# GpSimd's turns of an expert stage, thirty of them written out and without marks

## The reference

```python
def expert_block(args):
    xb, e = args
    gu = xb @ w_gate_up[e] + b_gate_up[e]
    gate = jnp.minimum(gu[:, 0::2], SWIGLU_LIMIT)
    up = jnp.clip(gu[:, 1::2], -SWIGLU_LIMIT, SWIGLU_LIMIT)
    act = (up + 1.0) * gate * jax.nn.sigmoid(SWIGLU_ALPHA * gate)
    return act @ w_down[e] + b_down[e]
...
out = jnp.zeros((T, D), jnp.float32).at[row_tok].add(ys.astype(jnp.float32) * row_w[:, None])
```

## Time and profile before

| | |
|---|---|
| median of three runs | 1679.5 us |
| span of the profiled execution | 1674.4 us |
| that execution's own device time | not given beside its span |
| PE busy | 1620.8 us, 97% of the span |
| POOL busy | 280.7 us, 17%, 355 instructions |
| moved by DMA | 489.80 MB, 293 GB/s in the mean |

### The profile page before, as it was taken

How to read it: one execution, slowest core, us unless ns; L and a number is a source line. 1 busy time by engine, 2 the same in 40 slices (tenths; PEclk the granted TensorE clock), 3 DMA queues, 4 the chain that set the end, 5 groups by cost and what they waited for, 6 DMA issues and landing times.

```text
span 1674.4 us, 44999 instructions
## 1 busy us (share of the span) xinstructions
PE 1620.8 (97%) x19112; PEld 900.9 (54%) x19112; DVE 577.2 (34%) x1341; ACT 423.4 (25%) x869; POOL 280.7 (17%) x355
## 2 busy tenths in 40 slices
PE   8999896999999989999999999999999999999996
PEld 6668896677888843344334433443443344334433
DVE  2448464755345553122212211321222132113212
ACT  4343433675223402121112111111211121111111
POOL 4000620101000020221211122111212211221211
PEclk9999999999999989999999999999999999999998
DMA  9940000312345479999999999999999999999983
GB/s 392 363 185 1 3 5 11 122 55 101 114 138 201 164 302 377 403 401 398 398 393 403 397 397 394 400 396 387 404 355 394 389 404 399 393 401 401 399 341 122
DMA packets 87479, 489.80 MB, mean 293 GB/s; under 512 B 15093, under 2 KB 17202, under 8 KB 34504
## 3 DMA queue, kind: packets, MB, share of 16 engines
q1 hardware_dynamic: 79708, 471.54, 70.8%
q0 software_dynamic: 7504, 16.80, 4.3%
q10 hardware_dynamic: 188, 0.30, 0.0%
HBM read 478.61 MB, written 19.55 MB: 298 GB/s over the span
## 4 chain that ended last, share of the span: by engine, by line
PE 63%; DVE 0%; issue 0%; POOLq 0%; DVEq 0%
PE bank L2324 39%; PE bank L2335 19%; PE bank L2315 2%; PE bank L2348 1%; PE bank L2336 1%; PE bank L2325 1%; DVE sb_y L2561 0%; PE bank L2358 0%; DVE sb_biased L2542 0%; POOLq L2201 0%; PE bank L2368 0%; PE bank L2363 0%; DVE sb_aT L2538 0%; DVE sb_aT L2539 0%; DVEq L2606 0%
## 5 line engine op out<-in xcount | busy, mean ns | idle before, releaser
L2324 PE MATMUL bank<-sb_w_raw,sb_xT 128*32 128x512 f32 x4554 | 665.4, 594 | 0.4 <-DVE sb_biased L2542 0.4
L2325 PE MATMUL bank<-sb_w_raw,sb_xT 128*32 128x512 f32 x1518 | 664.5, 594 | 0.0
L2324 PEld LDWEIGHTS bank<-sb_w_raw,sb_xT 128*32 128x32 f32 x4554 | 184.3, 110 | 431.2 <-issue 425.7
L2335 PE MATMUL bank<-sb_w_raw,sb_aT 128*32 128x256 f32 x4608 | 337.9, 379 | 2.0 <-DVE sb_aT L2539 2.0
L2336 PE MATMUL bank<-sb_w_raw,sb_aT 128*32 128x256 f32 x1536 | 337.5, 380 | 0.0
L2335 PEld LDWEIGHTS bank<-sb_w_raw,sb_aT 128*32 128x32 f32 x4608 | 187.7, 110 | 130.9 <-DVE sb_y L2561 2.3
L2542 DVE TENSOR_TENSOR sb_biased<-bank,sb_bias 128x512 f32<-128x512 f32 x96 | 60.3, 684 | 476.3 <-PE bank L2325 364.4
L2336 PEld LDWEIGHTS bank<-sb_w_raw,sb_aT 128*32 128x32 f32 x1536 | 166.3, 110 | 0.0
L2325 PEld LDWEIGHTS bank<-sb_w_raw,sb_xT 128*32 128x32 f32 x1518 | 164.5, 110 | 0.0
L2440 ACT COPY sb_bias<-sb_last_quarter 32x1536 f32<-32x1536 f32 x32 | 47.0, 1468 | 403.9 <-POOL sb_last_quarter L2497 403.9
L2492 POOL TENSOR_TENSOR sb_tick<-sb_ones 128x1 f32<-128x1 f32 x93 | 34.0, 366 | 557.4 <-issue 424.6
(11 more groups left out here) (512 smaller groups left out, 2245.1 us busy)
## 6 DMA issues: line engine op xcount, KB each, us to landing
sb_w_raw<-in_w_gate_up_dram SPq DMA_DIRECT2D x253, 1024.0 KB, 19.2
sb_w_raw<-in_w_down_dram SPq DMA_DIRECT2D x128, 1024.0 KB, 20.4
sb_ring<-in_w_in_dram SPq DMA_DIRECT2D x7, 2048.0 KB, 13.5
sb_x<-in_ada_w_dram SPq DMA_DIRECT2D x8, 1024.0 KB, 9.3
sb_mod<-in_ada_w_dram SPq DMA_DIRECT2D x8, 1024.0 KB, 8.0
sb_ring<-in_ada_w_dram SPq DMA_DIRECT2D x6, 1024.0 KB, 14.4
sb_x<-in_x_dram SPq DMA_DIRECT2D x2, 2048.0 KB, 9.6
sb_ring<-in_w_out_dram SPq DMA_DIRECT2D x2, 2048.0 KB, 7.5
```

Of the source, the lines that this page charges most:

```text
L2324: te.matmul(up_bank[r][at, :], g.xT[:, k, at], raw[:, s, 512 * r:512 * r + 512], start=first, stop=last)
L2325: mm = te.matmul(up_bank[r][CAP:P, :], g.xT[:, k, STRIP * r:STRIP * r + STRIP], raw[:, s, 512 * G:2048], start=first, stop=last)
L2335: te.matmul(down_bank[j][at, 0:256], g.aT[:, k, at], g.w_raw[:, s, 1024 * r + 256 * j:1024 * r + 256 * j + 256], start=first, stop=last)
```

## The change

Turns 0 to 29 of GpSimd (`LEAST_JOBS - 2` is 30) are written out one behind the other by Python's loop. In them all waits are for constants, and there are no marks. The runtime loop stays for turns from 30 on, with its three marks and waits for them; the values that it awaits on `ticked` count from the loop's own start. The wait for `out_set` moves from ahead of each add to ahead of turn 0, and the one behind the loop goes. `pool.again()` only resets a count that checks the order of names while the program is built; it makes no instruction.

```diff
@@ -2505,23 +2505,35 @@
             gather_rows(g, po, g.row_of[0:CAP, 1:2])
             po.wait_ge(*pe.credit())
             gather_rows(g, po, g.row_of[0:CAP, 2:3])
-            with po.Fori(0, last) as turn:
-
+            def turn_of_rows(turn):
                 po.wait_ge(g.row_in, 16 * turn + 32)
                 po.wait_ge(*vec.before("ad2", turn))
                 po.wait_ge(*act.before("quarter", turn))
-                po.wait_ge(ticked, 3 * turn + 1)
+                spread().then_inc(*pool("spread"))
+                po.wait_ge(*vec.at("row", turn))
+                gather_rows(g, po, g.row[0:CAP, 0:1])
+                po.wait_ge(*vec.at("y", turn))
+                add_rows(g, po, g.row_now[0:CAP, 0:1], y_out)
+
+            po.wait_ge(out_set, 16 * NT)
+            for turn in range(LEAST_JOBS - 2):
+                pool.again()
+                turn_of_rows(turn)
+            with po.Fori(LEAST_JOBS - 2, last) as turn:
+                pool.again()
+                po.wait_ge(g.row_in, 16 * turn + 32)
+                po.wait_ge(*vec.before("ad2", turn))
+                po.wait_ge(*act.before("quarter", turn))
+                po.wait_ge(ticked, 3 * turn + 1 - 3 * (LEAST_JOBS - 2))
                 tick(2)
                 spread().then_inc(*pool("spread"))
                 po.wait_ge(*vec.at("row", turn))
-                po.wait_ge(ticked, 3 * turn + 2)
+                po.wait_ge(ticked, 3 * turn + 2 - 3 * (LEAST_JOBS - 2))
                 tick(0)
                 gather_rows(g, po, g.row[0:CAP, 0:1])
                 po.wait_ge(*vec.at("y", turn))
                 tick(1)
-                po.wait_ge(out_set, 16 * NT)
                 add_rows(g, po, g.row_now[0:CAP, 0:1], y_out)
-            po.wait_ge(out_set, 16 * NT)
             po.wait_ge(*last_vec.at("y"))
             add_rows(g, po, g.row_now[0:CAP, 0:1], last_stored)
 
```

## The result

| | median us | runs | lowest to highest |
|---|---|---|---|
| before | 1679.62 | 20 | 1676.51 to 1682.56 |
| after | 1682.51 | 20 | 1679.01 to 1685.45 |

The ratio is 1.0015, with a 95% interval of 1.0009 to 1.0022: by the medians 2.9 us slower, and by the bound of 0.2% no change. The forecast was 1682.7 us.

A forecast was written before the change was run, and what follows sets the result against it. PE was taken to bound the steady part, hiding GpSimd's work; three switches in turn 30 (9.4, 8.6, 10.7, summing to 28.7 us) make the last scaling 3.2 us later: 1682.7 us against 1679.5, range 1679.2 to 1686.8.

The forecast's parts named there:

- Turns 0 to 29 at nothing: Written-out turns: some 20 us of GpSimd's time a turn removed, costed at nothing because PE's 985.60 us hide it.
- The wait for the output's stores at nothing: Wait moved ahead of turn 0's broadcast: over by 648.3, before the broadcast's present start at 649.57, so no cost.
- Turn 30: Loop's one turn: three GpSimd switches in a row instead of two, last scaling at 1666.7 against 1663.48, 3.2 us later.
- first switch: Ahead of tick(2) in turn 30, behind turn 29's add: 9.4 us, taken from turn 0; bounds 8.65 and 12.84.
- tick(2) to broadcast: Second switch, in turn 30: 8.6 us, taken from turn 0, putting the broadcast at 1639.5, 6.6 us late.
- row to tick(0): Third switch, turn 30, from DVE's row to tick(0): 10.7 us, against 11.45 in the kernel before.
- I take their middle: Third switch, ahead of tick(0) in turn 30: put at 10.7 us, between the extremes 8.65 and 12.84.
- Short switches: Rival, turn 30: three switches sum to 25.5 us or less, so the add is hidden and time stays 1679.5; chance 0.18.
- Long switches: Rival, turn 30: switches of 12.84, 10.5 idle and 12.84 give +10.8 us, 1690.3; later than 5.5 us has chance 0.12.
- Faster: Rival: GpSimd's queue was holding something, so earlier gathers and adds or fewer switches free PE; 1678.1 at best; chance 0.04.
- Not doing what it says: Rival, written-out turns: something else wants the ticks' kind, so a switch stays and time is 1679.5; nothing changed, chance 0.04.
- SP's loads of the last job: Tail: four loads go out 8.27 us behind turn 30's broadcast, last landing by 1661.2; taken as about even, no price.

The follow-up runs named there:

- the lower clock in one tail: Kernel before with its loop over all turns, its marks made by semaphore increments on GpSimd's queue: 1682.05 us, ratio 1.0016; PE's last product ran at clock 0.86.
- the closing ticks: One tick's product behind GpSimd's loop, added to the changed kernel and the kernel before, both with marks as queue increments: 1679.65 us (0.9992) and 1679.29 us (0.9996).

## Why the prediction was right

*Turns 0 to 29 at nothing.* Shown: 985.61 of 985.61 us for 30 turns, the same 32.85 us each, with 48 us less work on POOL and its switches gone. The adds start 0.8 us behind y (1622.31 + 0.48 to 1623.61 for turn 29).

*The wait for the output's stores at nothing.* The broadcast of turn 0 did wait for these stores, up to 647.33 us, in a stage that begins 3.7 us later. Counted in the stage that is 5.9 us before the old start (647.33 less 3.7, against 649.57), so the wait was over in time, as said. The opening took 53.03 us for 53.02.

*Turn 30.* By its own terms, measured in the trace after:

| term | predicted us | measured us |
|---|---|---|
| y of turn 29 to the add's end | 2.45 | 2.29 |
| first switch | 9.4 | 8.77 |
| tick(2) to broadcast | 8.6 | 7.67 |
| broadcast to row | 8.37 | 8.35 |
| row to tick(0) | 10.7 | 12.74 |
| tick(0) to add | 1.99 | 1.99 |
| add to share | 5.70 | 5.46 |
| share to scaling | 0.4 | 0.22 |
| sum, y to last scaling | 47.6 | 47.5 |

The sum holds to 0.1 us by luck of signs: the first two switches were put 1.6 us too long together, the third 2.0 too short. The mis-sized step is "I take their middle", the reasoning that 11.45 in turn 30 lies high among the 31 and would fall back. It doesn't fall back: in the six traces with a tick(0) in turn 30 that term is 11.45 to 12.74 us (12.0 in the mean). The last job's four loads go out just ahead of it each time; that they are what makes it long is likely, but no run shows it. A value that belongs to a place is better than the middle of all places. The first two switches lie where the weights' loads end and have ended (DMA share 0.63 and 0.09), and were shorter than the rows of turn 0 from which they were taken.

*The rivals.* Short switches: they sum to 29.2 us, over the 25.5 from which they would be hidden. The Trainium skill, "GPSIMD Engine Reference", section 2.1 Instruction dispatch, gives about 6 us for the first call into newly loaded code. Only the shortest switches of these traces come near that (5.83 us with no DMA beside it, 5.94 in the earlier trace rows); on the path here they took 7.5 to 12.7. Long switches: only the third was long, close to the largest of the 31, and the first two were short, so one made up for the other. Faster: refuted by the loop of before without switches, where nothing is won. Not doing what it says: refuted by the count of eight.

*SP's loads of the last job* went out at 1646.89, 5.37 us behind the broadcast and not 8.27. They cost nothing: PE's last product ended 24.80 us behind the last features both times (1663.35 less 1638.55, 1667.04 less 1642.24).

*The cause is shown,* not only argued: moving one of the three switches under a wait gives the time back, adding two lengthens the tail by about their idle time, moving the three one turn ahead of the end nearly hides them, and the written-out turns without switches cost nothing. What is open: the lower clock in one tail, and what exactly sets a switch's length.

## What to carry to other kernels

Work that one removes from an engine off the path is worth nothing until its last piece reaches the end, so look at the two edges of the stage before the long middle: here thirty turns of some 20 us saved on GpSimd brought nothing, and one added switch in turn 30 cost 3 us. When a stretch that alternates between two kinds of GpSimd's work is split into one kind and then the other, the change of kinds moves to the seam; put the seam where the engine waits anyway (one tick ahead of a wait took the loss back), or early enough that the turns behind it make up for it. Read a stall's price at the very place where it will stand, with the transfers that run beside it there.

## What the runs showed of the hardware

- GpSimd's kind outlasts the execution. With marks that make no compute instruction, the program's last compute instruction is a broadcast, and the next execution's first mask stood idle 12.30 and 12.07 us instead of 0.49; one tick's product as the last compute instruction brought the 0.49 back. Without that tick both kernels were 0.16% above before, with it 0.08% and 0.04% below, which can't be told from no change. Read off is the link of end and start. The pair of MODIFY_POOL_CONFIG at that mask is there in either case, as at tick(2) in the loop of before; that the loaded code is what stays would fit this, but no run shows it.
- A switch to the ticks' kind took 7.0 us with the DMA engines idle, 7.9 at a busy share of 0.33 (the closing ticks), 8.8 at 0.63, 12.6 at 0.70, 11.7 at 0.76, and 12.0 at 0.99, at the start; one to the broadcast's kind took 5.8 us with them idle and 7.5 at 0.09. In the steady turns, at 1.00, the two range from 8.65 to 12.84 and from 5.94 to 10.5, so the share alone doesn't set it.
- An indirect DMA and a memset run without a switch under either kind: the DMA starts 0.2 us behind either, and the first memsets stand at 0.29 to 1.04 us whether the mask behind them switches or not. An increment of a semaphore on GpSimd's queue served as a mark with no switch at all.
